# Who reads the turned attention weights of the local attention, and where layer 0's gate and modulation pieces stand between attention steps

## What is computed

```python
shift, scale, gate = split(silu(c) @ w_ada + b_ada, 3)      # the modulation
h = x * (1 + scale) + shift
(..., g_lat) = split(h @ w_in)                              # g_lat: the gate
y_a = recurrence(...)
y_b = softmax(q k^T) v                                      # global, 4 heads
y_c = (softmax(q1 k1^T) - lam * softmax(q2 k2^T)) v         # differential, 4 heads
y_d = softmax(banded q k^T, context, sink) v                # local window, 4 heads
y = concat(y_a, y_b, y_c, y_d) * silu(g_lat)
x_new = layer_norm(alpha * x + gate * (y @ w_out))
```

## Time and profile before

| | |
|---|---|
| median of 3 runs | 2167.43 us (2165.4 to 2173.59) |
| the profiled execution, its own time | 2162.25 us |
| its span | 2160.4 us |
| mean granted TensorE clock | 0.987 |
| PE busy | 94% |
| DVE busy | 53% |
| ACT busy | 36% |

### The profile page before, as it was taken

The page is one execution under the profiler, slowest core; times in us unless marked ns, Lnnn a source line. Parts: engine busy times, 40 slices in busy tenths (PEclk is TensorE's granted clock), DMA queues, the critical chain, the costliest instruction groups (busy, mean ns, idle before and its releaser), DMA issues.

```text
span 2160.4 us, 27157 instructions
## 1 busy us (share of the span) xinstructions
PE 2026.5 (94%) x10380; PEld 1430.8 (66%) x10380; DVE 1153.4 (53%) x2484; ACT 782.2 (36%) x1671; POOL 54.4 (3%) x96
## 2 busy tenths in 40 slices
PE   6989999999889999898998889999999999999999
PEld 2565464555547665564565678885888878888887
DVE  1655127556657848216676787967444435333333
ACT  2132123455452323123564443346322324222222
POOL 2000000000000000000000200000000000000000
PEclk9999999999999999999999999999999999999999
DMA  9111010101444211112000323230333331333331
GB/s 298 30 59 39 25 63 8 32 1 40 157 162 118 79 49 39 39 49 78 1 1 30 103 68 98 79 88 1 88 97 96 95 103 49 98 98 98 97 94 63
DMA packets 152687, 157.32 MB, mean 73 GB/s; under 512 B 5676, under 2 KB 114384, under 8 KB 152560
## 3 DMA queue, kind: packets, MB, share of 16 engines
q1 hardware_dynamic: 146672, 137.91, 20.8%
q0 software_dynamic: 5888, 17.68, 2.9%
HBM read 151.37 MB, written 4.19 MB: 72 GB/s over the span
## 4 chain that ended last, share of the span: by engine, by line
PE 73%; DVE 17%; ACT 4%; issue 3%; DMA 2%; POOL 1%; DVEq 0%; ACTq 0%; SPq 0%; POOLq 0%
PE psum L807 11%; PE psum L1300 10%; PE psum L1302 10%; PE psum L1301 10%; PE psum L993 6%; PE psum L819 6%; PE psum L835 5%; PE psum L1008 3%; PE psum L1027 3%; PE psum L768 2%; DVE arena L2450 2%; DVE stats L2161 1%; ACT arena L1414 1%; PE psum L853 1%; PE psum L781 1%
## 5 line engine op out<-in xcount | busy, mean ns | idle before, releaser
L1414 ACT ACTIVATE arena<-psum 128x384 f32<-128x384 f32 (+5 forms) x510 | 199.6, 420 | 596.3 <-PE psum L768 171.5
L1300 PE MATMUL psum<-part,part 128*128 128x512 f32 x992 | 387.8, 391 | 5.2 <-DVE part L2565 2.7
L1302 PE MATMUL psum<-part,part 128*128 128x512 f32 x992 | 387.3, 390 | 0.0
L1301 PE MATMUL psum<-part,part 128*128 128x512 f32 x992 | 387.2, 390 | 0.0
L807 PE MATMUL psum<-arena 128*128 128x512 f32 (+1 forms) x960 | 319.2, 488 | 0.8 <-ACTq L1417 0.8
L1414 ACT ACTIVATE part<-arena 128x1024 fp32r<-128x1024 f32 (+1 forms) x214 | 190.6, 924 | 225.8 <-PE psum L1302 150.0
L2565 DVE TENSOR_TENSOR part<-arena,part 128x1024 fp32r<-128x1024 f32 x112 | 137.1, 1226 | 252.1 <-ACT part L1414 252.1
L807 PEld LDWEIGHTS psum<-arena 128*128 128x128 f32 x960 | 178.7, 190 | 120.6 <-issue 105.4
L1300 PEld LDWEIGHTS psum<-part,part 128*128 128x128 f32 x992 | 186.5, 188 | 45.7 <-DVE part L2565 3.1
L1302 PEld LDWEIGHTS psum<-part,part 128*128 128x128 f32 x992 | 186.7, 188 | 39.2
L1301 PEld LDWEIGHTS psum<-part,part 128*128 128x128 f32 x992 | 186.7, 188 | 39.1
(11 more groups left out here) (279 smaller groups left out, 2392.3 us busy)
## 6 DMA issues: line engine op xcount, KB each, us to landing
arena<-in_w_in SPq DMA_DIRECT2D x75, 512.0 KB, 4.0
arena<-in_w_mlp SPq DMA_DIRECT2D x64, 512.0 KB, 3.8
arena<-in_w_ada SPq DMA_DIRECT2D x48, 512.0 KB, 5.6
arena<-in_w_gate SPq DMA_DIRECT2D x32, 512.0 KB, 4.0
arena<-in_w_out SPq DMA_DIRECT2D x24, 512.0 KB, 3.9
arena<-in_w_in SPq DMA_DIRECT2D x16, 256.0 KB, 3.4
arena<-in_w_branch SPq DMA_DIRECT2D x8, 512.0 KB, 3.7
arena<-in_x POOLq DMA_DIRECT2D x4, 512.0 KB, 9.2
```

Source lines behind the costliest of these rows:

```text
L1300: pe.matmul(dst, lo, x_hi_, start=first, stop=False)
L1301: pe.matmul(dst, hi, x_lo_, start=False, stop=False)
L1302: return pe.matmul(dst, hi, x_hi_, start=False, stop=last)
L1414: return act.activation(dst, src, ACT.Copy)
```

## The change

It has three parts. First, `by_act` gives the turned groups of the local attention out by head: ACT reads both groups of head 0, DVE both of head 1, in both layers, and ACT reads its two groups ahead of its exponentials. Second, layer 0's list of pieces is written out by hand: the 24 gate pieces go behind rounds 0 to 3, the odd rounds 5 to 15, and 17 to 30. Third, a modulation part is cut in five pieces (products 0-1, 2-3, 4-5, 6-7, then the transposes), and two pieces stand behind each of rounds 31 to 50; ACT's copy is at the fourth piece, DVE's reduction at the fifth.

```diff
--- before.py
+++ after.py
@@ -576,9 +576,9 @@
 
             n = len(attention_steps(l)) + 4
             if l < DEPTH - 1:
-                total = 4 * last_q_of(l) + (16 if l < DEPTH - 1 else 0)
-                upto = [-(-i * total // n) for i in range(n + 1)]
-                return [upto[i + 1] - upto[i] for i in range(n)]
+
+                ones = {0, 1, 2, 3, 5, 7, 9, 11, 13, 15} | set(range(17, 31))
+                return [1 if i in ones else 2 if 31 <= i < 51 else 0 for i in range(n)]
             else:
                 ones = {0, 1, 2, 3, 5, 7, 9, 11, 13, 15} | set(range(24, 30))
                 return [1 if i in ones else 0 for i in range(n)]
@@ -649,7 +649,9 @@
 
         def by_act(kind, i, half):
 
-            return kind == "c" or half == 0 if kind in "cd" else (i + half) % 2 == 0
+            if kind in "cd":
+                return kind == "c" or i == 0
+            return (i + half) % 2 == 0
 
         def turn_read(l, k, i, half):
             return (pt_act if by_act(attention_steps(l)[k][0], i, half) else pt_dve).at("t", l, k, i, half)
@@ -781,6 +783,8 @@
                         mm = pe.matmul(bank(0)[g:g + 32, :], csil[:, 2 * k:2 * k + 32], ring.view("ada", l, n, k // 2)[:, k % 2, :], start=k < 4, stop=k >= 4)
                         if k % 2:
                             mm.then_inc(mm_done(("weights", ring.number("ada", l, n, k // 2))), 1)
+                            if k < KT - 1:
+                                yield True
                     bank_free(0, [ada_act.at("row", l, n)])
                     yield True
                     b = 6 + n % 2
@@ -1419,6 +1423,8 @@
 
             def ada(parts_):
                 for p, (l, n) in enumerate(parts_):
+                    for _ in range(KT // 2 - 1):
+                        yield True
                     if (l, n) == (0, 4):
                         act.wait_ge(*rows_pool.at("q", "d", 0, TT - 1))
                     act.wait_ge(*mm_done.at("weights", ring.number("ada", l, n, KT // 2 - 1)))
@@ -1621,11 +1627,12 @@
                     turns = []
                     if 0 <= i - 2 < len(steps_):
                         turns = [x for x in turns_of(l, i - 2) if by_act(steps_[i - 2][0], *x)]
-                        read_turned(l, i - 2, turns[0:1], banks)
+                        ahead = 2 if steps_[i - 2][0] == "d" else 1
+                        read_turned(l, i - 2, turns[0:ahead], banks)
                     if i < len(steps_):
                         exps(l, i)
                     if turns:
-                        read_turned(l, i - 2, turns[1:], banks)
+                        read_turned(l, i - 2, turns[ahead:], banks)
                     if 0 <= i - 3 < len(steps_) and steps_[i - 3][2] == last_e(steps_[i - 3][0]):
                         read_heads(l, i - 3)
                     if l < 2 and len(steps_) - 1 <= i < len(steps_) + 2:
@@ -1971,7 +1978,8 @@
 
             def ada(parts_):
                 for l, n in parts_:
-                    yield True
+                    for _ in range(KT // 2):
+                        yield True
                     dve.wait_ge(*turn_done.at("ada", l, n))
                     bias = cols_a[:, 24 + 24 * l + 4 * n:24 + 24 * l + 4 * n + 4]
                     sums = ada_t[:, l, 4 * n:4 * n + 4, :]
```

## The result

The changed kernel takes 2152.87 us (median of 5 runs, 2142.24 to 2154.48) where the kernel before takes 2167.43 (median of 5, 2165.40 to 2173.59; three of these were known ahead of the prediction). The medians are 14.6 us apart, and the forecast was 2152.0. The ratio over all runs is 0.9925, with a 95% interval of 0.9906 to 0.9943, which is 16.3 us.

A forecast was written before the change was run, and what follows sets the result against it. PE's own work was taken as the main bound, leaving its waits to win: layer 1 -8.2 and layer 0 -7.3 make -15.5 us, 2151.9 against the median 2167.43, forecast as 2152.0. Range 2143 to 2157, whole range 2141 to 2164.

The forecast's parts named there:

- groups by head in layer 1: Layer 1's local steps and last rounds: reads given out by head shorten PE's waits for shared banks, -8.2 us.
- step 31 and the last rounds: End of layer 1's attention: 1.76 us from the odd step and 1.0 from the last rounds.
- Even steps: Layer 1's local steps 26, 28 and 30: shorter waits give 0.7 us in step 26, 1.9 in all.
- Layer 0's heads: Layer 0's steps 38 to 43 and last rounds: same gains as layer 1, less DVE's small operations, together -7.5 us.
- The gate's list: Layer 0's rounds 0 to 30: 3.85 us come off early, 3.25 come back later, net -0.6, ends -3.9 and +1.6.
- The modulation's price on PE: Layer 0's cut modulation: lone pairs of products at 0.93 us add +3.7, seams of twelve more bursts +1.2.
- The new waits: Layer 0's rounds 35, 38, 40, 45 and 50: transposes wait for ACT or DVE, +5.0 us, bounds 2 and 10.
- What the pieces give back: Layer 0: pieces lie where PE sat, -5.6 us behind even rounds and -2.5 in rounds 34, 43 and 47.
- The clock: Layer 0's local steps and last rounds: fewer waits remove some half-clock time, -1.0 us, from 0 to -6.
- The half gain: Local steps of both layers: DVE becomes late, odd steps give 0.9 us, new waits reach 4; 2161 us, chance 0.25.
- The slower case: Layer 0's local steps: pieces make PE stop and go at half clock, +30 us, 2189 in all, chance 0.07.
- The far better one: Layer 0: all half-clock spells go and new waits stay lowest, 2143 us; within the forecast's case, no chance of its own.

The follow-up runs named there:

- experiment 7: Kernel before with only the hand-written list of the 24 gate pieces, modulation whole and where it was: 2163.74 us beside 2166.79, ratio 0.9982.
- Experiment 1: Kernel before with only the turned groups of the local attention given out by head: 2154.75 us beside 2167.15, ratio 0.9931.
- experiment 3: Changed kernel with the modulation in whole parts at its old rounds: 2148.50 us beside 2167.15, ratio 0.9904.
- Experiment 4: Changed kernel with a list that keeps a part's last piece and its transposes out of one round: 2146.16 us beside 2167.15, ratio 0.9894.
- experiment 5: Kernel of experiment 4 with ACT reading a third turned group ahead of its exponentials: 2144.99 us beside 2166.79, ratio 0.9905.
- experiment 6: Kernel of experiment 4 with DVE reading its turned groups of a local step ahead of settling the sums: 2143.92 us beside 2166.79, ratio 0.9898.
- experiment 8: Changed kernel run once more with another profile, nothing altered: 2151.70 us beside 2166.79, ratio 0.9927.
- experiment 9: Kernel of experiment 4 with the reads of experiments 5 and 6 and a list also keeping transposes out of round 41: 2140.56 us beside 2166.49, ratio 0.9878.
- experiment 10: Kernel of experiment 3, modulation in whole parts, with the reads of experiment 9: 2147.48 us beside 2166.49, ratio 0.9909.
- experiment 2: Changed kernel with the turned groups read as before, keeping the new list and the modulation pieces: 2170.71 us beside 2167.15, ratio 1.0005.

## Why the prediction was right, and where not

**The total** was right: 15.5 us were forecast, 14.6 measured in the medians, and 14.6 to 15.4 in the profile once the spell at 391.34 is left out, at 1.7 or 0.9. Over half of it was right for the reason given. The rest is in part luck: layer 0's heads gave less than was said and the gate's list more, by some 2 us each. The step at the centre, groups by head in layer 1, was forecast at 8.2 and is 8.04. In step 27 the mechanism is exact: heads at +4.85 forecast, +4.87 measured; a gain of 1.76 forecast, 1.74 measured; the next late thing is DVE's copy, as said. Its sum, though, holds two errors that cancel. Step 29 gained 3.35 and not 1.76, because in before PE fell to half clock behind the 1.44 us wait for ACT (timeline of PE, before), and in the changed kernel it did not:

```profile
1183.40 0.69 PE L768 MATMUL psum<-ident,arena 128*128 128x128 f32 x2 [1.44 <-ACT arena L1414]
1183.88 3.33 PE L819 MATMUL psum<-arena 128*128 128x512 f32 x4
```

These gate products take 1.88 at full clock, so 1.45 of the 3.35 is the clock's. It belongs to the change all the same: experiment 7, with the old reads, has the same four gate products in 3.32 us behind the same wait of 1.44 and the stage at 49.72 us (before: 49.75), and no kernel with the new reads has it over 42.21 (experiments 1, 3 to 6 and 8 to 10). The forecast named no such term for layer 1. On the other side, step 31 and the last rounds were to give 2.8 (1.76 and 1.0) and gave 0.48. The changed kernel, the same view:

```profile
1175.25 1.80 PE L997 MATMUL psum<-arena 64*128 64x256 f32 x8 [0.41 <-ACT arena L1597]
...
1180.11 0.44 PE L770 MATMUL psum<-ident,arena 128*128 128x128 f32 x2 [0.43 <-DVE arena L2183]
...
1183.76 0.66 PE L1012 MATMUL psum<-ident,arena 128*128 128x128 f32 x4 [1.12 <-ACT arena L1418]
1184.96 0.65 PE L1012 MATMUL psum<-ident,arena 128*128 128x128 f32 x4 [0.54 <-DVE arena L2183]
```

The heads of step 31 are turned 4.86 us behind its scores, 1.5 sooner than the 6.39 of before, and the turning of the next weights then waits 1.12 for ACT and 0.54 for DVE: that gives it back. What keeps ACT is on record too (timeline of ACT, the changed kernel):

```profile
1180.98 1.28 ACT L1645 ACT_TABLE_LOAD   x1
1182.27 1.06 ACT L1645 ACTIVATE arena<-arena 128x1024 f32<-128x1024 f32 x1
1183.24 0.91 ACT L1418 ACTIVATE arena<-psum 128x384 f32<-128x384 f32 x3
```

The table load before the SiLU rows and the first of these rows, 2.3 us together, stand ahead of the next copy out of a shared bank. PE comes to that bank sooner than before and only waits longer for the same copy. The forecast named the SiLU rows and gave them no wait. No run moves them. Even steps gained 2.5 (0.95, 1.41 and 0.11) where 1.9 was said.

**Layer 0's heads**, "together -7.5", was mis-sized. Experiment 1 shows -4.7, and experiments 7 and 3, which differ in the reads alone, -5.3 (112.07 and 106.75). The shape was the same as in layer 1, and steps 40 to 43 do gain 6.2; but step 38 gained nothing, being held by ACT's exponentials. And the step left out that in this stretch the clock drops and moves, so that PE at half clock in step 39 took back what the missing waits gave, and the last rounds lost 0.95 where 1.0 was to come.

**The gate's list**, -0.6, was too cautious. Rounds 0 to 15 took 71.46, 0.8 less than forecast, and rounds 16 to 30 grew by 1.0 us for three pieces, with nothing added in 31 to 36 in experiment 7. The forecast had 3.25 come back, and only 1.0 did. PE's idle time between the scores of steps 16 and 31 fell from 3.2 to 0.8 us, and its busy time rose by 3.4, less than the 5.4 of three pieces. Experiment 7's numbers, 2.0 to 2.8 (profile, without the spell), 3.1 (medians) and 3.9 (ratio), lie between the forecast and its -3.9 end.

**The modulation's price on PE** was right in what it counted. What a lone pair takes no row had shown, and 0.93 was taken between 0.46 and 1.9. A burst is what stands of the modulation's products between two other instructions of PE. Two bursts of the changed kernel, timeline of PE:

```profile
540.56 1.06 PE L783 MATMUL psum<-arena,csil 128*32 128x512 f32 x8
541.55 0.70 PE L997 MATMUL psum<-arena 64*128 64x256 f32 x4
...
547.19 1.05 PE L783 MATMUL psum<-arena,csil 128*32 128x512 f32 x4
548.18 0.44 PE L973 MATMUL psum<-ident,arena 128*128 128x128 f32 x2
```

Four instructions and eight both take 0.99 us to the start of the next. Twenty bursts of 0.99 are 19.8, against 8 parts of 1.86 = 14.9: the +3.7 and +1.2 of the forecast, 4.9, measured 4.9 by this count. The Trainium skill's page TensorEngine Tiling (Tiling Modes) has four tiles of 128x32 side by side, which agrees with this trace: eight instructions in 0.99, where four of the gate's take 1.88. The forecast saw no row of the drain by itself; the trace has it. Transposes, which use the whole array, and then a burst of the modulation, in two narrow windows of the timeline of PE:

```profile
582.77 0.49 PE L1012 MATMUL psum<-ident,arena 128*128 128x128 f32 x3
```

```profile
582.99 0.27 PE L1012 MATMUL psum<-ident,arena 128*128 128x128 f32 x1
583.19 1.05 PE L783 MATMUL psum<-arena,csil 128*32 128x512 f32 x4
```

The three transposes start 0.11 us apart (582.77, 582.88, 582.99), and the burst starts 0.20 behind the last of them. So a change of mode costs 0.09 us here. The Trainium skill's page TensorEngine Tiling (Key Properties) states that changing the tiling mode drains the engine; it gives no size, and the trace agrees. The change behind a burst is within its 0.99 us, the one ahead is not: 16 of the 20 bursts stand behind instructions of the whole array, where 6 of the 8 whole parts did. By this estimate the pieces cost PE some 0.9 us more than the 4.9.

**The new waits**, 5.0 in sum, were in the places named. In the changed kernel, rounds 38 and 40, timeline of PE, and ACT ahead of the second:

```profile
571.34 0.66 PE L770 MATMUL psum<-ident,arena 128*128 128x128 f32 x4 [1.36 <-DVE arena L2183]
...
583.19 1.05 PE L783 MATMUL psum<-arena,csil 128*32 128x512 f32 x4
586.58 0.63 PE L770 MATMUL psum<-ident,arena 128*128 128x128 f32 x4 [2.33 <-ACT arena L1418]
...
625.93 0.66 PE L770 MATMUL psum<-ident,arena 128*128 128x128 f32 x4 [1.93 <-ACT arena L1418]
```

```profile
585.21 0.47 ACT L1601 ACTIVATE stats<-sinks,stats 128x1 f32<-128x1 f32 x2
585.58 0.86 ACT L1418 ACTIVATE arena<-psum 128x256 f32<-128x256 f32 x2
```

ACT comes to the modulation's bank only behind exponentials and sinks, as argued: its copy is the second of the two from 585.58. Round 40 waits 2.33 us (1.7 forecast, with the transposes in it), round 38 1.36 (1.0), rounds 35, 45 and 50 0.79 each (0.9, 0.7, 0.7). The wait of 1.93 in round 48 was not foreseen; ACT's table load (at 622.76) and first SiLU row stand ahead of the copy there, as in layer 1. Experiment 4 took away the four waits for ACT in rounds 35, 40, 45 and 50, 4.7 us, for one new wait of 1.67, and gained 3.4. What the other two, 1.36 and 1.93, cost by themselves no run shows.

**What the pieces give back**, -8.1, holds in part. In round 36 the products do lie where PE sat: the step is as long with 0.99 us of them as with the 1.86 of experiment 3 (4.11 and 4.10). But rounds 34, 38 and 43, which have no piece in experiment 3 and were to take theirs for nothing, grew by 1.00, 1.50 and 2.29 us; of the 1.50, the wait of 1.36 is counted above.

**The clock** was forecast at -1.0, from 0 to -6. The time at half clock fell from 17 to 3 us, more than said, and experiment 3 (clock 0.89, 106.75 us) suggests that this only pays for the new waits. That gives +1.8 - 1.0 in the forecast and -0.2 to +0.2 in the profile (106.57 against 106.75 and 106.41). By the medians of experiment 3 and the changed kernel the pieces cost up to 4.4, so the net of pieces and clock, forecast at +0.8, stays open between -0.2 and +4.4.

**The rivals.** The half gain needed DVE to be late in layer 1's odd steps, at 0.9 gained a step: they gained 1.74 and 3.35. The slower case needed PE at half clock through the stage: the clock rose. The far better one, 2143, came true only for single runs, and not in the place it named: the profiled run of 2142.24 differs from that of 2151.99 behind layer 1.

What stays open: why the spells at half clock fall where they do. In experiments 5, 6, 9 and 10 layer 1's last rounds took 18.0 to 20.4 us and not 16.3, at a clock of 0.75 to 0.91; the wait behind the SiLU rows, 1.12 us in the changed kernel, was 1.4 to 1.9 in them. Whether the longer wait brings the half clock was not tried apart.

## What to carry to other kernels

Of several groups that leave shared banks, let the engine that is idle first read the one whose bank is needed first, and look at which copy is late next before adding more. Cut a side stream into pieces only so that its producer, its copy and its consumer fall into different rounds, and count what the cut costs: with old reads the same pieces cost 6.6 us of a stage, with new reads nothing in the profile and perhaps 4 in the median, with the hand-over moved by one round they gave 3.6 (experiments 4 and 3), and in the best order 5.3, about half of it the clock's. Look also at what an engine does behind its last round: 2.3 us of a table load and a SiLU row ate what the last rounds were to give. Compare stage by stage, from one instruction to the same one, before setting one profiled execution against another.

## What the runs showed of the hardware that was not expected

The time at half clock depends on how the work is cut, not only on how much PE idles. With PE's work in this stretch nearly the same (68.5 and 66.8 us busy), the whole parts gave a mean clock of 0.89 (experiments 1 and 3) and the pieces 0.98, with idle times of 12.3 and 12.4 us. With the old reads the cut made no such difference: 0.92 for whole parts (experiment 7) and 0.93 for pieces (experiment 2). The Trainium skill's page TensorE: Matmul & The Clock Gate (What's actually happening), by which the clock follows how busy the engine was, agrees in sense with the spells that begin behind waits (at 575.55 behind 1.98 us in experiment 1, at 1183.88 behind 1.44 in before); but why other waits as long brought none (2.33 us at 586.58 in the changed kernel, at full clock behind it), no run here shows.

A change of tiling mode on TensorE costs 0.09 us, and a pair of the modulation's products (four instructions) takes as long as two pairs, 0.99 us: in this kernel a piece of two products costs PE what a piece of four does.

And the runs of one kernel, with every attention stage equal to 0.05 us, can differ by 10 us (2142.24 and 2151.99), for a mean clock of 0.995 and 0.988.
